# RWKV-7 chunk inverse on packed 32x32 diagonal blocks, decay products side by side, weight products in quarters

## The reference

```
def step(state, inp):
    r_t, w_t, k_t, v_t, a_t, b_t = inp
    sa = einsum('bhij,bhj->bhi', state, a_t)
    state = (state * w_t[:, :, None, :] + sa[..., None] * b_t[:, :, None, :]
             + v_t[..., None] * k_t[:, :, None, :])
    return state, einsum('bhij,bhj->bhi', state, r_t)
```

## Time and profile before

| | |
|---|---|
| median of 3 runs | 3332.87 us (3327.38 to 3342.9) |
| the profiled execution, its own time | 3329.62 us |
| its span, first to last instruction | 3327.8 us |
| PE busy | 3242.5 us, 97% of the span |
| DVE busy | 1774.2 us, 53% |
| ACT busy | 1247.7 us, 37% |
| POOL busy | 193.2 us, 6% |
| mean granted TensorE clock | 0.992 of 2.4 GHz |

### The profile page before, as it was taken

The page is one execution under the profiler, slowest core; times in us unless marked ns, Lnnn a source line. Parts: engine busy times, 40 slices in busy tenths (PEclk is TensorE's granted clock), DMA queues, the critical chain, the costliest instruction groups (busy, mean ns, idle before and its releaser), DMA issues. The chain is left out here.

```text
span 3327.8 us, 52710 instructions
## 1 busy us (share of the span) xinstructions
PE 3242.5 (97%) x22179; PEld 2664.4 (80%) x22179; DVE 1774.2 (53%) x2970; ACT 1247.7 (37%) x1967; POOL 193.2 (6%) x156
## 2 busy tenths in 40 slices
PE   7999999999999999989999999999999999999999
PEld 6877777777777787867788888888888888888887
DVE  5235555545555455363436777433656566655832
ACT  4124343433333332242325666323334344443421
POOL 1000000001001111100000111010000000000000
PEclk9999999999999999999999999999999999999999
DMA  7433333331212134332442122443332233322552
GB/s 234 114 82 87 86 98 92 87 109 48 62 54 83 57 113 146 95 114 76 111 110 80 45 58 86 130 145 108 89 89 89 76 95 94 96 89 76 165 143 85
DMA packets 492528, 324.30 MB, mean 97 GB/s; under 512 B 27130, under 2 KB 448605, under 8 KB 491782
## 3 DMA queue, kind: packets, MB, share of 16 engines
q1 hardware_dynamic: 492294, 320.94, 33.3%
HBM read 276.05 MB, written 44.85 MB: 96 GB/s over the span
## 5 line engine op out<-in xcount | busy, mean ns | idle before, releaser
L534 PE MATMUL PS<-XH,WHT 128*128 128x512 f32 (+1 forms) x2224 | 897.7, 404 | 7.1 <-DVE AR L1031 2.1
L522 DVE TENSOR_TENSOR WLT<-AR,WHT 128x1024 fp32r<-128x1024 f32 (+1 forms) x430 | 527.3, 1231 | 667.2 <-ACT WHT L516 666.8
L536 PE MATMUL PS<-XH,WLT 128*128 128x512 f32 (+1 forms) x2224 | 872.6, 392 | 0.0
L516 ACT ACTIVATE WHT<-AR 128x1024 fp32r<-128x1024 f32 (+1 forms) x430 | 446.9, 1042 | 646.6 <-PE PS L536 483.5
L535 PE MATMUL PS<-XL,WHT 128*128 128x512 f32 (+1 forms) x1712 | 671.2, 392 | 0.0
L534 PEld LDWEIGHTS PS<-XH,WHT 128*128 128x128 f32 (+1 forms) x2224 | 417.5, 188 | 109.2 <-issue 10.8
L536 PEld LDWEIGHTS PS<-XH,WLT 128*128 128x128 f32 (+1 forms) x2224 | 417.7, 188 | 96.2
L535 PE MATMUL PS<-ARR,WHT 128*128 128x512 f32 x1024 | 404.6, 395 | 0.0
L535 PEld LDWEIGHTS PS<-XL,WHT 128*128 128x128 f32 (+1 forms) x1712 | 321.7, 188 | 71.7 <-issue 4.6
L535 PEld LDWEIGHTS PS<-ARR,WHT 128*128 128x128 f32 x1024 | 192.4, 188 | 40.4 <-issue 0.2
L534 PE MATMUL PS<-XL,WHT 128*128 128x512 f32 x512 | 203.3, 397 | 0.1
(11 more groups left out here) (487 smaller groups left out, 5336.5 us busy)
## 6 DMA issues: line engine op xcount, KB each, us to landing
AR<-b_w_in SPq DMA_DIRECT2D x128, 512.0 KB, 4.0
AR<-w_in SPq DMA_DIRECT2D x122, 512.0 KB, 4.1
AR<-a_w_in SPq DMA_DIRECT2D x48, 512.0 KB, 4.4
AR<-w_out SPq DMA_DIRECT2D x32, 512.0 KB, 4.8
AR<-a_w_out SPq DMA_DIRECT2D x32, 512.0 KB, 4.0
AR<-b_w_out SPq DMA_DIRECT2D x32, 512.0 KB, 4.1
proj_scratch<-AR SPq DMA_DIRECT2D x33, 256.0 KB, 2.0
AR<-a_w_kv_up SPq DMA_DIRECT2D x32, 256.0 KB, 3.7
```

Of the source, the lines that this page charges most:

```text
L516: self.nc.scalar.activation(self.shaped(self.high, n), self.shaped(self.raw, n), ACT.Copy).then_inc(self.s_high, 1)
L522: self.nc.vector.tensor_tensor(self.shaped(self.low, n), self.shaped(self.raw, n), f32(self.shaped(self.high, n)), ALU.subtract).then_inc( ...
L534: mm(out, wh, xh[k0 + c], start=(start and c == 0), stop=False)
L536: last = mm(out, wl, xh[k0 + c], start=False, stop=(stop and c == nk - 1))
```

## The change

1. The first five levels of the inverse (m = 1 to 16) stay inside the 32x32 diagonal blocks. The change keeps only these blocks, packed to 32 columns a chunk (`TD`, `LOT`, `X`, `GD`), and multiplies each with a matmul of 32 rows, 32 weight columns and 32 moving columns, at partitions 64e + 32b (`sub(e, b)`). The last level computes only the off-diagonal 32x32 block, and the whole inverse is put together in `TF`. `lower` makes both the lower blocks and their transposes.
2. Products and sums of a half share one bank, B[h]; so B[2] and B[3] are free during the levels, and the two products of `decays` go there, one right behind the other, without the wait between them.
3. `piece` issues a quarter of a unit (6 matmuls). Four stand ahead of level 1, and at levels 2 to 5 there is one between `products` and `sums` and one behind `sums`.
4. DVE's and ACT's operations on these are half as wide, POOL makes 4 masks instead of 5, DVE adds a copy (`GD`) and two products with a mask of one column (`diagonal`).

The core of the diff:

```diff
-    def matmuls(self, pe, n, bank, xh, xl, k0, start, stop, part=None):
+    def matmuls(self, pe, n, bank, xh, xl, k0, start, stop, part=None, parts=2):
-        if part != 1:
+        if part in (None, 0):
-        for c in range(nk) if part is None else range(nk // 2 * part, nk // 2 * part + nk // 2):
+        for c in range(nk) if part is None else range(nk // parts * part, nk // parts * (part + 1)):
-        if part != 0:
+        if part in (None, parts - 1):
...
-    X = take(T).rearrange("p (c f) -> p c f", f=CH)
+    X, GD = (take(T // 2).rearrange("p (c f) -> p c f", f=SB) for _ in range(2))
-    TT = take(2 * T).rearrange("p (h j c f) -> p h j c f", h=2, j=2, f=CH)
+    TD = take(T).rearrange("p (j c f) -> p j c f", j=2, f=SB)
+    TF = take(T).rearrange("p (c j f) -> p c j f", j=2, f=SB)
-    LOT = [x.rearrange("p (c f) -> p c f", f=CH) for x in (take(T), take(T))]
+    LOT = [x.rearrange("p (c f) -> p c f", f=SB) for x in (take(T // 2), take(T // 2))]
...
-    def lev(n, c=NCH):
-        return C("lev", n * CH, (n + 1) * CH).unsqueeze(1).broadcast_to([P, c, CH])
+    def sub(e, b):
+        return slice(64 * e + SB * b, 64 * e + SB * b + SB)
+    def stok(c, b):
+        return slice(c * CH + b * SB, c * CH + b * SB + SB)
+    def at(c, j=0):
+        return slice((j * HC + c) * SB, (j * HC + c + 1) * SB)
+    def lev(n):
+        return C("lev", n * SB, (n + 1) * SB).unsqueeze(1).broadcast_to([P, NCH, SB])
...
             for i in range(NPAIR):
-                for l in levels:
+                for l in levels[:-1]:
                     if l == 1:
-                        G.wait(pool, i, "dve.gb3")
-                        S.wait(pool, i - 1, f"pe.x1{NL - 1}")
+                        G.wait(pool, i, "dve.gd")
+                        S.wait(pool, i - 1, f"pe.x1{LAST - 1}")
                     elif l > 2:
                         S.wait(pool, i, f"pe.x1{l - 2}")
-                    S.did(nc.gpsimd.tensor_tensor(LOT[l % 2], GB[:, :, 0, :], lev(l + 1), ALU.mult), "pool", f"lot{l}")
+                    S.did(nc.gpsimd.tensor_tensor(LOT[l % 2], GD, lev(l + 1), ALU.mult), "pool", f"lot{l}")
         @block.tensor
         def _(pe):
...
+                u = unit(i, j // 4)
                 if u is None:
                     return
                 t = u // 2
-                if u % 2 == 0 and j % 2 == 0 and t > first:
+                if u % 2 == 0 and j % 4 == 0 and t > first:
                     pe.wait_ge(evac_d, t - first)
-                st.matmuls(pe, u, B[FBK], k.XHT, k.XLT, 8 * (u % 2), u % 2 == 0, u % 2 == 1, j % 2)
+                st.matmuls(pe, u, B[FBK], k.XHT, k.XLT, 8 * (u % 2), u % 2 == 0, u % 2 == 1, j % 4, 4)
             def out_half(n, part):
...
                         pe.wait_ge(ld, i * 80)
                     else:
                         pe.wait_ge(w_t, 1)
-                    N.wait(pe, i - 1, "act.tokA")
-                else:
-                    N.wait(pe, i, "act.sgw")
-                N.did(mm(B[6][:, :], W2[rows(e), :], TW[rows(e), :], start=True, stop=True), "pe", ("zw", "za")[e])
+                N.did(mm(B[2 + e][:, :], W2[rows(e), :], TW[rows(e), :], start=True, stop=True), "pe", ("zw", "za")[e])
             def key_sums(i):
                 N.wait(pe, i, "act.sqk")
-                if i:
-                    N.wait(pe, i, "act.sga")
+                N.wait(pe, i - 1, "act.tokA")
                 for b in range(TB):
                     last = mm(B[6 if i else 5][:, 2 * b:2 * b + 2], SQN[:, blk(b)], C("cmask"), start=True, stop=True)
                 N.did(last, "pe", "ss")
...
             def lower(i):
                 S.wait(pe, i - 1, "dve.qt")
-                G.did(each(range(NCH), lambda c, e: mm(B[0][rows(e), tok(c)], AR[rows(e), 0, tok(c)], SQN[rows(e), tok(c)], start=True, stop=True)), "pe", "lm")
+                for j in range(2):
+                    for c in range(NCH):
+                        for b in blocks:
+                            for e in heads:
+                                x, y = AR[rows(e), 0, stok(c, b)], SQN[rows(e), stok(c, b)]
+                                last = mm(B[0][sub(e, b), j * T // 2 + c * SB:j * T // 2 + (c + 1) * SB], (x, y)[j], (y, x)[j], start=True, stop=True)
+                G.did(last, "pe", "lm")
             def products(i, l):
                 for h in halves:
-                    S.wait(pe, i, f"pool.lot{l}")
                     if l == 1:
                         G.wait(pe, i, "dve.t0b")
                         S.wait(pe, i - 1, "dve.qt", f"dve.su{NCH - 2}")
                     else:
                         S.wait(pe, i, f"dve.ta{h}{l - 1}")
-                    S.did(each(range(HC), lambda c, e: mm(B[h][rows(e), tok(c)], LOT[l % 2][rows(e), HC * h + c, :], TT[rows(e), h, 0, c, :], start=True, stop=True)), "pe", f"x{h}{l}")
+                    if l < LAST:
+                        S.wait(pe, i, f"pool.lot{l}")
+                        for c in range(HC):
+                            for b in blocks:
+                                for e in heads:
+                                    last = mm(B[h][sub(e, b), at(c)], LOT[l % 2][sub(e, b), HC * h + c, :], TD[sub(e, b), 0, HC * h + c, :], start=True, stop=True)
+                    else:
+                        last = each(range(HC), lambda c, e: mm(B[h][sub(e, 1), at(c)], GB[sub(e, 0), HC * h + c, 0, SB:CH], TD[sub(e, 0), 0, HC * h + c, :], start=True, stop=True))
+                    S.did(last, "pe", f"x{h}{l}")
             def sums(i, l):
                 for h in halves:
                     S.wait(pe, i, f"act.xc{h}{l}")
-                    def one(c, e, n=1):
-                        x, tt = X[rows(e), HC * h + c, :], TT[rows(e), h, 1, c, :]
-                        if n:
-                            return mm(B[2 + h][rows(e), tok(HC + c)], x, tt, start=True, stop=True)
-                        return mm(B[2 + h][rows(e), tok(c)], tt, x, start=True, stop=True)
-                    S.did((both if l < NL - 1 else each)(range(HC), one), "pe", f"t{h}{l}")
+                    if l < LAST:
+                        for c in range(HC):
+                            for j in range(2):
+                                for b in blocks:
+                                    for e in heads:
+                                        x, t = X[sub(e, b), HC * h + c, :], TD[sub(e, b), 1, HC * h + c, :]
+                                        last = mm(B[h][sub(e, b), SB * HC + SB * (HC * j + c):SB * HC + SB * (HC * j + c + 1)], (t, x)[j], (x, t)[j], start=True, stop=True)
+                    else:
+                        for c in range(HC):
+                            for b in blocks:
+                                for e in heads:
+                                    x, t = X[sub(e, 1), HC * h + c, :], TD[sub(e, 1), 1, HC * h + c, :]
+                                    last = mm(B[h][sub(e, b), at(c, 2)], (x, C("eye32")[sub(e, 1), :])[b], t, start=True, stop=True)
+                    S.did(last, "pe", f"t{h}{l}")
             def value_scores(i):
...
-                    S.wait(pe, i, f"dve.ta{h}{NL - 1}")
-                    S.did(each(range(HC), lambda c, e: mm(B[h][rows(e), blk(c)], TT[rows(e), h, 1, c, :], TOK[rows(e), 0:2, HC * h + c, :], start=True, stop=True)), "pe", f"pt{h}")
+                    S.wait(pe, i, f"dve.ta{h}{LAST}")
+                    S.did(each(range(HC), lambda c, e: mm(B[h][rows(e), blk(c)], TF[rows(e), HC * h + c, :, :], TOK[rows(e), 0:2, HC * h + c, :], start=True, stop=True)), "pe", f"pt{h}")
...
             decays(0, 0)
+            decays(0, 1)
             ahead(2)
-            decays(0, 1)
             key_sums(0)
...
             ahead(7)
             for i in range(NPAIR):
                 more, tail = i + 1 < NPAIR, i > 0
-                piece(i, 0)
-                piece(i, 1)
+                for j in range(4):
+                    piece(i, j)
                 if not more:
                     out_half(0, 0)
                 for l in levels:
                     products(i, l)
                     if l > 1:
-                        piece(i, l)
+                        piece(i, 2 * l)
                     if not more and l in (2, 4):
                         out_half(l // 2 - 1, 2 - l // 2)
                     sums(i, l)
...
                         value_scores(i)
                     if l == 1 and tail:
                         centred(i - 1)
-                    if l in (2, 3) and more:
-                        decays(i + 1, l - 2)
+                    if l == 2 and more:
+                        decays(i + 1, 0)
+                        decays(i + 1, 1)
                     if l == 3 and tail:
                         variances(i - 1)
                     if l == 4 and more:
                         key_sums(i + 1)
+                    if l > 1:
+                        piece(i, 2 * l + 1)
                 solved(i)
-                piece(i, 6)
+                piece(i, 12)
+                piece(i, 13)
```

(43 more changed lines are left out.)

19 lines of the change are left out of this document (12 added, 7 removed).

## The result

The changed kernel takes 3343.3 us (median of 20 runs, 3337.2 to 3353.4), the one before 3333.3 (20 runs, 3324.9 to 3342.9): ratio 1.0035, 95% interval 1.0025 to 1.0046. It is 10 us slower, inside the 0.5% that counts as no change and inside the range given, but 49 us above the 3294 that were forecast and on the other side of the kernel before. The profiled execution took 3338.83 us.

What follows compares the result with a forecast made beforehand. PE, busy 97% of the span, was taken as the bound. Terms -40.8 - 8 + 5.2 + 2 + 2 + 2 - 1.1 = -38.7 us gave 3290.9 from the profiled 3329.6, 3294 for the median; range 3272 to 3355.

Steps and rivals of the forecast that it cites:

- The record: Inverse: 32x32 records at four places 8.1 ns each, at two 16.3, against 29.2 before; -5.1 us a pair.
- A: Rival, inverse: only two places work at a time, every record costs 16.3 ns; 3353 us, chance 0.13.
- B: Rival, inverse: a fixed price per record, not under 29 ns; 3455 us (3422 at 25 ns), chance 0.07.
- The breaks: Pieces cut into quarters: 26 more breaks between large and small matmuls at 0.2 us each, +5.2 us.
- it is the array and not the issue that binds: Inverse's 64x64 records: the array sets their 29.2 ns, since at half the clock 32 take 1.97 us against 1.15.
- C: Rival, inverse: something between, such as the array's queue not fed every 8 ns; at 14 ns a record 3335 us, chance 0.09.
- The decays: The two decay matmuls overlap, so one of two vanishes: -1.0 us, 8 times, -8 us.
- rival E: Clock: 32x32 records use a quarter of the array, each pair gets a half-clock stretch; +28 us, 3322, chance 0.05.
- Large matmuls now stand on both sides of every burst: Clock: the argument given against a half-clock stretch of 7 us in each pair, +3.5 us each.
- The signs to look for: Levels: burst lengths, decays within 1.2 us, clock 1.00 in pairs 0 to 4; wrong if idle before bursts exceeds 4 us a pair.
- terms of work in the sum: PE's work: inverse -40.8 us, decays -8, breaks +5.2, going between 32x32 and 64x64 records +2.
- terms of waiting: PE's waits: handovers at level 1 +2 us, handovers without quarters +2, pair 7's start -1.1.

Runs made afterwards that it cites:

- e8: Kernel before, with the two decay products side by side and the inverse's last level on its one nonzero 32x32 block: 3327.4 us.
- e1: Kernel before, with the pieces cut into quarters and nothing else (64x64 inverse, decays one by one): ratio 1.0032.
- e6: Changed kernel, with both quarters of a half again between products and sums: 3353.7 us.
- e7: Kernel before, with only the two decay products side by side, through banks 6 and 7 behind the sums of level 2: ratio 0.9984.
- e5: Kernel before, with 4 more large matmuls in each pair's second piece: clock cost +10.7 us, remaining time +4.9 us.
- e13: Kernel before with two quarters inside the chain, plus 4 large matmuls a pair: clock cost +2.0 us, remaining time +7.6, against the same without those matmuls.
- e15: Kernel before with two quarters inside the chain, plus ACT's level 1 copy repeated eight times: clock cost +13.9 us, remaining time +20.0, against it without repeats.

## Why the prediction failed

- **The record** was nearly right: 8.1 ns was assumed for four places, 0.5 us and 1.05 us for 64 and 128 records; measured are 8.9 ns, 0.57 and 1.13 us, and A and B fell. The Trainium skill (page TensorE: Matmul & The Clock Gate, Back-to-back issue gap) has small matmuls start no closer than about 25 ns; across four places the trace disagrees, with eight records begun in 0.06 us (891.31 to 891.37). The 16.3 ns for two places held in e8 (5.8 us for 6.6).
- **The breaks** had the right steps in and out (0.32 and 0.34) and the wrong price: e1's rest grew by 2.0 where 26 breaks were put at 5.2, and e6 says 2.3.
- **The step that failed first** is "it is the array and not the issue that binds". It was read from bursts of 64x64 records, which use up their instructions 3.3 times as slowly (29.2 ns for 8.9). C had the thought, "the queue in front of the array not being fed", but as a price for every record, decided at 14 ns. In truth a record costs 8.9 ns until the block ends, and then PE stands still for 0.1 to 4.1 us: 32.2 us in all, a wait that the sum put at nothing. Pair 1 shows both: 44.20 us before, 42.02 now, and without its three stops (0.37, 0.38 and 1.71 us) 39.6, that is -4.6, for the -4.8 a pair of the sum.
- **The decays** were right in what they cost (1.06 for two) and wrong as a term: -8 us left out what the second of them covered. In e7 the rest fell by 2.2 in place of 8.5, and in the pair looked at 0.72 of 1.06 us came back as a wait.
- **The clock** was rival E, at 28 us with a chance of 0.05; by the split it cost 27.3. The size was luck: E gave every pair the same stretch at half clock, while the profiled execution has 0.97 for 0.99 up to pair 6 and 0.86 for 0.94 behind. The ground given, that 32x32 records use a quarter of the array, is not what e1, e5 and e13 show for the chains, but those are 2.8 of the 27.3 us. Of the other 24.5 the stops can make 20 at most, by e15's rate; whether the records themselves cost the rest, or more, is open. "Large matmuls now stand on both sides of every burst" does not hold where it mattered, at levels 4 and 5 of pair 6 and in most of pair 7.
- **The signs to look for** were well chosen for A and B and blind to the rest: PE's idle time before `products` and `sums` was to stay under 4 us a pair, and on average it did (25 us in 8 pairs), though not in pairs 0, 6 and 7 (4.1, 4.5 and 5.3); the forecast was lost below that mark. The sign to name was the sum over all pairs, and what it may not exceed.

By the sum: -38.7 + 32.2 (stops) + 2.5 (the wait for bank 4) = -4.0 of the rest, where -15.0 was measured over the runs. The stops are those of one execution, and the split puts too much on the clock, so the two profiled executions alone add up better. PE was busy 3242.5 and 3222.1 us, of these 38.7 and 73.6 at half the clock. Counted at the full clock, its work is 3223.2 and 3185.3, that is -37.9, where the terms of work in the sum make -41.6 (-40.8 - 8 + 5.2 + 2). Its idle time is 85.3 and 114.9, +29.6, where the terms of waiting make +2.9. The lower clock made its work 19.4 and 36.8 longer, +17.5. Together that is the +9.2 of the two spans. So the work came out within 4 us of its terms, and what failed are the stops and the clock. Over the runs the changed kernel ends 12 us above the kernel before by means, 10 by medians.

## What to carry to other kernels

Small matmuls side by side can be fast (8.9 ns a record at four places, for 29.2 with 64x64 at two), but each is as much instruction as a large one: count a stretch's PE instructions (four for every f32 matmul) in blocks of 256, and if PE uses up a block in less than about 4 us, expect it to stop at the end: 25 of the 29 stops followed blocks that PE had used up within 3.2 us. Before moving an instruction, ask what it covered where it stood, the evacuation of a bank included. Put some large matmuls into every stretch in which PE has only small ones and waits: here that was worth 16 us without any other change, and in the one test of it (e13) work added elsewhere no longer cost clock. Look first at the stretches that have no large matmuls to give: here nearly all the loss stood in the last two pairs.
